# Two blocks of a hybrid network on one core: decay rows in two matmuls per head, gate columns by transposes, a root spread by fp32r products

## The reference, cut to what matters

```python
# rms_norm, before each projection and each feed-forward part
y = xf * rsqrt(mean(xf * xf, axis=-1) + eps) * gain

# first block, LSTM heads (4 heads of 64), chunk by chunk
b = cumsum(log_sigmoid(f_pre))                 # sum of log forget gates
d = b[t] - b[s] + i[s]   (s <= t, else -inf)   # log decay from token s to token t
m_t = maximum(b + m, max_s d)
w_intra = exp(d - m_t)
qk = (q @ k.T) * w_intra
h = (... qk @ v ...) / maximum(abs(den), exp(-m_t))
```

## Time and profile before

| | us |
|---|---|
| median of the three runs | 1680.75 |
| span of the profiled execution | 1678.3 |
| PE busy | 1657.2 |
| DVE busy | 1236.7 |
| ACT busy | 989.4 |
| POOL busy | 189.3 |

### The profile page before, as it was taken

One profiled execution on the slowest core, in us unless ns is written; L12 is line 12 of the kernel. 1 busy time (PEld: TensorE's weight loads), 2 busy tenths in 40 slices (PEclk: granted clock), 3 DMA queues, 4 the chain that ended last, 5 costly groups with the idle time before them and its releaser, 6 DMA issues.

```text
span 1678.3 us, 25649 instructions
## 1 busy us (share of the span) xinstructions
PE 1657.2 (99%) x9974; PEld 1449.4 (86%) x9974; DVE 1236.7 (74%) x1982; ACT 989.4 (59%) x1656; POOL 189.3 (11%) x173
## 2 busy tenths in 40 slices
PE   7999999999999999999999999999999999999999
PEld 5788888878888888888888988888888888998888
DVE  7787765778776567876677878767776677778774
ACT  5776654577665455554577665545554467765542
POOL 2620000162100000000521000000000242100000
PEclk9999999999999999999999999999999999999999
DMA  7626555542755555556534555555555643355553
GB/s 283 202 103 212 179 210 196 210 146 102 263 180 210 193 196 188 188 201 248 204 102 147 181 191 185 201 204 193 181 199 200 252 165 127 139 184 192 198 201 126
DMA packets 62014, 313.97 MB, mean 187 GB/s; under 512 B 22681, under 2 KB 24349, under 8 KB 25286
## 3 DMA queue, kind: packets, MB, share of 16 engines
q1 hardware_dynamic: 60374, 303.92, 51.1%
q0 software_dynamic: 1232, 4.22, 0.8%
q10 hardware_dynamic: 288, 4.19, 0.7%
HBM read 311.24 MB, written 7.36 MB: 190 GB/s over the span
## 4 chain that ended last, share of the span: by engine, by line
PE 97%; ACT 2%; DVE 0%; DMA 0%; SPq 0%; issue 0%; DVEq 0%; ACTq 0%
PE acc L417 46%; PE acc L419 23%; PE acc L406 4%; PE acc L408 4%; PE acc L407 4%; PE acc L426 3%; PE acc L427 2%; PE acc L428 2%; PE tp L830 1%; PE tp L814 1%; PE acc L573 1%; ACT work L863 1%; PE sc L803 1%; PE acc L803 0%; PE sc L948 0%; ACT prob L863 0%
## 5 line engine op out<-in xcount | busy, mean ns | idle before, releaser
L392 DVE TENSOR_TENSOR w_lo<-raw,w_hi 128x1024 fp32r<-128x1024 f32 (+1 forms) x564 | 679.9, 1213 | 295.2 <-ACT w_hi L383 293.3
L383 ACT ACTIVATE w_hi<-raw 128x1024 fp32r<-128x1024 f32 (+1 forms) x564 | 583.3, 1039 | 185.6 <-PE acc L419 120.0
L417 PE MATMUL acc<-act_a,w_hi 128*128 128x512 f32 x1440 | 505.8, 395 | 0.0
L417 PE MATMUL acc<-hidden,w_hi 128*128 128x512 f32 x1216 | 421.8, 392 | 0.0
L419 PE MATMUL acc<-act_a,w_lo 128*128 128x256 f32 x1440 | 401.7, 279 | 0.0
L419 PE MATMUL acc<-hidden,w_lo 128*128 128x256 f32 x1216 | 338.9, 279 | 0.0
L417 PEld LDWEIGHTS acc<-act_a,w_hi 128*128 128x128 f32 x1440 | 269.7, 187 | 63.4 <-issue 3.5
L417 PEld LDWEIGHTS acc<-hidden,w_hi 128*128 128x128 f32 x1216 | 227.6, 187 | 51.2
L419 PEld LDWEIGHTS acc<-act_a,w_lo 128*128 128x128 f32 x1440 | 271.5, 189 | 0.1
L591 ACT COPY part<-acc 128x256 f32<-128x256 f32 x272 | 101.3, 373 | 281.0 <-PE acc L419 279.7
L417 PE MATMUL acc<-act_b,w_hi 128*128 128x512 f32 x688 | 239.4, 392 | 0.0
(11 more groups left out here) (234 smaller groups left out, 2066.5 us busy)
## 6 DMA issues: line engine op xcount, KB each, us to landing
raw<-in_slabs SPq DMA_DIRECT2D x282, 1024.0 KB, 4.8
na_skew<-in_rpb SPq DMA_DIRECT2D x32, 128.0 KB
na_bias<-na_skew ACTq DMA_DIRECT2D x2, 2048.0 KB, 8.3
t_skew<-t_by_distance POOLq DMA_DIRECT2D x2, 1024.0 KB, 14.1
t_bias<-t_skew POOLq DMA_DIRECT2D x1, 2048.0 KB, 10.3
x_res<-in_x SPq DMA_DIRECT2D x1, 1024.0 KB, 4.9
out_x<-x_res SPq DMA_DIRECT2D x8, 128.0 KB, 5.0
prow<-in_prow SPq DMA_DIRECT2D x1, 518.0 KB
```

Of the source, the lines that this page charges most:

```text
L383: nc.scalar.activation(w_hi[u % RING][:, 0:n], raw[j % RAW][:, (u % 2) * HALF:(u % 2) * HALF + n], ACT.Copy).then_inc(s["unit_hi"], 1)
L392: nc.vector.tensor_tensor(w_lo[u % RING][:, 0:n], raw[j % RAW][:, (u % 2) * HALF:(u % 2) * HALF + n], w_hi[u % RING][:, 0:n].bitcast(F32), ...
L417: nc.tensor.matmul(bank[:, :], wh, src[:, c + i, :, :].rearrange("p i s -> p (i s)"), start=first and i == 0, stop=False, skip_group_check ...
```

## The change

- `decay(m)` on PE does two matmuls of 256 columns, one with `g_hi` and one with `g_lo`. The 128 columns of the first half of the queries are the first 128 of these, so DVE adds the mask in two instructions, 128 and 256 columns wide, from the same PSUM columns.
- `gate_columns()` on PE uses four transposes of a whole 128x128 tile. Their results lie 128 columns apart, and DVE's copy picks 4 columns of each.
- `dve_diag` makes two fp32r parts: `diag_hi` (rounded), and behind a wait for it `diag_lo` (the rest). `pe_bcast` multiplies an fp32r copy of the ones, `ones_r`, with both parts and adds them in PSUM.
- DVE makes `ones_r` once, between its first eight activation parts and its first weight split.

```diff
         ones_m = sb("ones_m", [P, P])
+        ones_r = sb("ones_r", [P, P], F32R)
...
-        diag = over("diag", [P, T, P])
+        diag_hi = over("diag_hi", [P, T, P], F32R)
+        diag_lo = over("diag_lo", [P, T, P], F32R)
...
             for t in range(T):
-                ins = nc.vector.tensor_scalar(diag[:, t, :], ident[:, :], rstd[:, t:t + 1], None, ALU.mult)
+                ins = nc.vector.tensor_scalar(diag_hi[:, t, :], ident[:, :], rstd[:, t:t + 1], None, ALU.mult)
+            tick(dve, b, dve_chain, ins)
+            for t in range(T):
+                ins = nc.vector.scalar_tensor_tensor(out=diag_lo[:, t, :], in0=ident[:, :], scalar=rstd[:, t:t + 1],
+                                                     in1=diag_hi[:, t, :].bitcast(F32), op0=ALU.mult, op1=ALU.subtract)
             ins.then_inc(s["diag_ready"], 1)
...
-            nc.tensor.matmul(tp[bank][:, 0:S], ones_m[:, :], diag[:, :, :].rearrange("p t s -> p (t s)"), start=True,
-                             stop=True).then_inc(tp_full[bank], 1)
+            nc.tensor.matmul(tp[bank][:, 0:S], ones_r[:, :], diag_hi[:, :, :].rearrange("p t s -> p (t s)"),
+                             start=True, stop=False)
+            nc.tensor.matmul(tp[bank][:, 0:S], ones_r[:, :], diag_lo[:, :, :].rearrange("p t s -> p (t s)"),
+                             start=False, stop=True).then_inc(tp_full[bank], 1)
...
                     for j in range(2):
-                        c = (2 * t + j) * LSTM
-                        mm = nc.tensor.matmul(tp[bank][:, c:c + LSTM], g_row[:, j, t * P:(t + 1) * P],
-                                              ident[:, 0:LSTM], start=True, stop=True)
+                        mm = nc.tensor.transpose(tp[bank][:, (2 * t + j) * P:(2 * t + j + 1) * P],
+                                                 g_row[:, j, t * P:(t + 1) * P], ident[:, :])
...
                 row = pick[:, m:m + 1].broadcast_to([P, P])
-                for to, w in ((slice(0, P), P), (slice(P, 3 * P), S)):
-                    nc.tensor.matmul(tp[bank][:, to], row, g_hi[:, 0:w], start=to.start == 0, stop=False,
-                                     skip_group_check=True)
-                    mm = nc.tensor.matmul(tp[bank][:, to], row, g_lo[:, 0:w], start=False, stop=to.start > 0,
-                                          skip_group_check=True)
-                mm.then_inc(tp_full[bank], 1)
+                nc.tensor.matmul(tp[bank][:, 0:S], row, g_hi[:, :], start=True, stop=False)
+                nc.tensor.matmul(tp[bank][:, 0:S], row, g_lo[:, :], start=False, stop=True).then_inc(tp_full[bank], 1)
...
-                nc.vector.tensor_copy(gcol[:, :, :, :].rearrange("p t i h -> p (t i h)"), tp[bank][:, 0:4 * LSTM])\
+                nc.vector.tensor_copy(gcol[:, :, :, :].rearrange("p t i h -> p (t i) h"),
+                                      tp[bank][:, :].rearrange("p (c k) -> p c k", k=P)[:, :, 0:LSTM])\
                     .then_inc(s["gcol_ready"], 1)
...
-                nc.vector.tensor_tensor(w1[:, m, :], tp[bank][:, 0:3 * P], mask_m[:, :], ALU.add)\
-                    .then_inc(s["d_seen"], 1)
+                for t in range(T):
+                    ins = nc.vector.tensor_tensor(w1[:, m, HALVES1[t]], tp[bank][:, 0:(t + 1) * P],
+                                                  mask_m[:, HALVES1[t]], ALU.add)
+                ins.then_inc(s["d_seen"], 1)
...
+            nc.vector.tensor_copy(ones_r[:, :], ones_m[:, :])
             dve_split(dve, b, 2)
```

## The result

Five runs of the changed kernel gave 1687.56 to 1690.94 us, median 1687.98, against 1680.75 before: a ratio of 1.0046 (95% interval 1.0036 to 1.0057). The forecast was 1678.1 with a range to 1679.7, so the sign is wrong. Four of the five lie within 0.6 us; the one at 1690.94 was not traced. The profiled span is 1686.0 us (before 1678.3).

A forecast was written before the change was run, and what follows sets the result against it. PE was taken to bound the kernel, 97% of the chain that ended last. Mixers −1.34, roots −1.44 and cast +0.15 sum to −2.63 us on 1680.75, giving 1678.1 us, range 1676.5 to 1679.7.

The forecast's parts named there:

- The step that failed: Feed-forward parts: PE runs without a gap, so what it saves at the spread roots reaches the end of the kernel.
- B: Rival: weight loads show in new matmul pairs; roots save nothing, gate columns and decay(0) keep about 0.67; 1679.6 us, chance 0.08.
- E: Rival: the diagonal comes late and PE waits at six feed-forward roots; 1682.9 us; chance 0.06 together with things unseen.
- the chance of 0.03 for slower: Whole kernel: time above 1684.1 us, given half of the 0.06 for a late diagonal and things unseen.
- Roots: Eight spread roots: an fp32r pair costs 0.24 us instead of 0.42, saving 0.18 each, 1.44 in all.
- Gate columns and first decay: First-block mixers: PE needs 0.68 us instead of 1.35; the 0.67 saved per layer reaches the end.
- Decay 1 to 3: First-block mixers: 0.22 us saved each, 0.66 per layer, all turned into PE waits at turn(0) and turn(1).
- The rival A: All PE savings pass, because DVE reaches the weighted scores earlier: 1676.8 us, chance 0.12.
- Net of all this: First-block mixers: of 1.33 us PE work saved per layer, 0.67 reaches the end, 1.34 in two layers.
- The cast: Kernel start: DVE's cast to ones_r delays the first weight split, adding 0.15 us; split at 11.92.
- C: Rival: the cast at the start costs 0.70 us, like the trace's only one; 1678.7 us, chance 0.06.
- Diagonal: Spread roots: DVE's low parts add 0.5 us, ready at 141.6 before PE comes at 142.44; hidden.

The follow-up runs named there:

- e1: Changed kernel with the root's single fp32 product, its diagonal and its cast as before; decay rows and gate columns stay changed: 1679.20 us, ratio 0.9989.
- e9: Changed kernel with all its added DVE root work, but PE multiplies an undivided diagonal in one fp32 product: 1680.00 us, ratio 0.9994.
- e10: Kernel before with only the gate columns turned by four transposes instead of four fp32 matmuls: 1680.30 us, ratio 0.9994.
- e11: Kernel before with only the decay rows in two matmuls and the mask in two pieces: 1680.26 us, ratio 0.9996.
- e12: Changed kernel with the fp32r pair only at the first block's two roots, a single fp32 product at the six others: 1679.55 us, ratio 0.9991.
- e2: Kernel before with the root part alone (two fp32r parts, ones_r, cast at the start): 1689.32 us, ratio 1.0047.
- e3: Changed kernel with both products of the diagonal's parts in fp32 instead of fp32r: 1688.22 us, ratio 1.0041.
- e5: Changed kernel with an unused two-column fp32 product behind each root's fp32r pair: 1691.67 us, ratio 1.0065.
- e6: Changed kernel with one fp32r product per root, the low part left out: 1686.64 us, ratio 1.0032.

## Why the prediction was wrong

**The step that failed** is the one from PE's saving at a root to the end of the kernel. The prediction put it so: PE bounds the kernel, in the feed-forward parts it "runs without a gap", so "a microsecond less on PE is worth a microsecond". That takes for granted that the stream behind an edited place keeps its pace. It does not: before, the single fp32 product took a slow stream to the quick pace at each root where it was needed. The pair keeps the slow pace, and three stretches of some 63 units pay 3.14, 3.13 and 3.17 us and the 0.19 that each root saves in them: 10.0 together. The sum had −1.44 for the eight roots. The products themselves gave −0.19 each, −1.5 in all, but the root part as a whole cost 8.8 us (1687.98 against 1679.20 in e1). With the gains of all other intervals this is the whole result: −0.15 − 0.88 − 0.10 − 0.23 − 0.21 − 0.22 + 3.14 + 3.13 + 3.17 = 7.65 us of 7.7 in the span. Before, e1, e9, e10, e11 and e12 have the single product at 34 feed-forward roots, and behind all 34 the stream is quick, in front of 16 of them slow; after, e2 and e12 have the pair at 14, and behind all 14 the pace is the one in front. (The pair met a slow front at 6 roots and the quick one of 346 and 347 ns at 8; what it does behind steps of 350 and 343 no run shows.) The untraced runs fit this. The runs of before, 62 in all, lie between 1680.19 and 1681.99, and those of each of e1, e9, e10, e11 and e12 within 1.7 us, less than one slow stretch costs. Among those of after, e3, e5 and e6 some lie 3 us and more apart, so there the slow stretches seem to differ from run to run.

None of the rivals had it. B asked whether weight loads come to light in the pair, and they do not: it steps at 0.12. By the rule of the Trainium skill that stood behind B ("TensorE: Matmul & The Clock Gate", section "The mechanism") the root would have kept its 0.42; the trace does not agree, with 0.24. The same section also names a background weight buffer into which a load may go ahead, and 0.24 does not contradict that. E asked whether the diagonal comes late, and it does not: `diag_lo` ends at 141.59, PE comes at 142.29. The slower result came without any wait, and the chance of 0.03 for slower stood for mishaps of the kinds that a waits view shows.

What would have warned: in the trace of before the step from a w_hi matmul to its w_lo matmul was 236 ns in front of the fifth and eighth root, and 230 behind them. The prediction read a pair's 0.35 once, at the first root, which is quick on both sides.

**The steps that held**, against before, unit by unit:

- Roots: −0.19 to −0.20 at each of the eight, from the last w_hi matmul in front to the second behind (1.13 before, 0.93 to 0.94 after), forecast −0.18.
- Gate columns and first decay: −0.65 per layer, forecast −0.67. e10 and e11 split it into 0.43 and 0.23.
- Decay 1 to 3: −0.23 each, and 0.66 and 0.63 given back in the two layers. e11 confirms that this belongs to the decay rows alone. The rival A, for which all of it passes, is refuted. But the place was half right. In the second layer only 0.36 comes at the turns, and 0.27 already in the gaps at 353.26, where PE meets the splits that DVE starts at 352.30. The prediction had followed only the next LSTM step and not the units in between.
- Net of all this: −0.58 in the first layer, if the start is taken as +0.43, and −0.70 in the second, forecast −0.67 each.
- The cast: the first split moved from 11.77 to 11.93, +0.16, forecast 0.15 (its row lasts 0.22). C is refuted.
- Diagonal: parts and wait end 0.65 us behind the diagonal's own end (140.47 + 0.47 to 141.59), forecast 0.5; hidden.

**Not settled.** What in TensorE makes the two paces is not shown. No view tells them apart but the steps: granted clock, loads, DMA share and waits are alike. Type (e3, e5), number of loads (e6) and DVE's work (e9) are excluded as the rule. That four products of 128 columns turned the pace over six times of six, while two fp32 products or three fp32r ones did so only in some stretches, fits a phase of the stream that the root's matmuls shift. That is an idea and not shown. The three steady patterns of the steps, and the four narrow matmuls that keep one quick pattern quick and turn the other slow at the third root, fit it too. Why the sixth root's front differs between kernels (the fifth's and eighth's is slow in all), and what differs between runs of one kernel, stays open.

**What to keep.** e1, decay rows and gate columns without the root part, is the fastest that was run, 1679.2 us, 0.1% below before, with an interval that ends just below 1. Between e1 and e12 nothing can be told.

## What to carry to other kernels

Where one engine bounds the kernel by a long stream of equal steps, look at the step itself on both sides of the place that you edit, to the nanosecond: a change of 2% in it over 60 units outweighs any instruction saved. Compare two traces from landmark to landmark before looking for waits; here that named the three stretches at once, while the chain and the waits looked unchanged. And when an engine upstream is dense, what the downstream one saves comes back at every hand-over behind it, the ordinary weight splits among them.

## What the runs showed of the hardware

- A stream of fp32r matmuls of 512 and 256 columns with a weight load each ran at 346.7 or 353.3 ns a pair, for 63 units on end, at a granted clock of 1.00 in both. The slow pace repeats 350, 361 and 349 ns, the quick one 346, 347 and 347 or 350 and 343. A few matmuls between two tiles decided which.
- The kernel's start varies. In before the first matmuls, 264 columns wide, step at 0.22 us until 15.36 and at 0.12 from then on; in after until 16.39, which cost 0.4 us. e1 and e11, without any cast, have 0.9 to 1.0 and 0.7 more at this place, and e12 1.0. The window view gives 1.00 as granted clock on both sides of the step. Differences under a microsecond between two traces are better read behind this place.
- An fp32 matmul of four columns is dearer than a transpose of 128: replacing four of them saved 0.43 us, and the four transposes take 0.35 (335.64 to 335.99).
